# A two-block transformer kernel: opening, attention order and the place of half units

## The reference

```
x = x + 0.5 * swiglu(rmsnorm(x), wg, wu, wd)        # 1024 -> 2816 -> 1024
h = rmsnorm(x) @ w_in
o = concat(mla_mixer(h_a), nsa_mixer(h_b), diff_mixer(h_c))
x = x + o @ w_out
x = x + 0.5 * swiglu(rmsnorm(x), wg2, wu2, wd2)
```

## Time and profile before

| | |
|---|---|
| Median of 3 runs | 1830.25 us (1827.8 to 1834.87) |
| The profiled execution | 1835.67 us |
| Its span, first to last instruction | 1833.9 us |
| Busy in the span | PE 1711.5, DVE 1158.1, ACT 867.2, POOL 112.8 us |
| PE's mean granted clock | 0.953 of full speed |

### The profile page before, as it was taken

One profiled execution on the slowest core, in us unless ns is written; L12 is line 12 of the kernel. 1 busy time (PEld: TensorE's weight loads), 2 busy tenths in 40 slices (PEclk: granted clock), 3 DMA queues, 4 the chain that ended last, 5 costly groups with the idle time before them and its releaser, 6 DMA issues.

```text
span 1833.9 us, 30713 instructions
## 1 busy us (share of the span) xinstructions
PE 1711.5 (93%) x12072; PEld 1567.2 (85%) x12072; DVE 1158.1 (63%) x1286; ACT 867.2 (47%) x1035; POOL 112.8 (6%) x89
## 2 busy tenths in 40 slices
PE   3999999999999799999999999979998979999997
PEld 3999978778999799997877899968997967787785
DVE  6655566446555465557544655557755758888887
ACT  3433443345343443443434544346643537666675
POOL 0000031001000100003100100001201000000000
PEclk9999999799999899999968999989988989999999
DMA  7655731024555655564102455635532368998993
GB/s 214 197 189 178 188 116 47 24 70 143 189 195 183 161 184 190 193 165 138 36 12 82 148 185 181 194 109 159 163 115 69 113 232 293 319 346 306 345 330 121
DMA packets 237690, 312.96 MB, mean 171 GB/s; under 512 B 50900, under 2 KB 176148, under 8 KB 237604
## 3 DMA queue, kind: packets, MB, share of 16 engines
q1 hardware_dynamic: 237604, 311.82, 52.5%
HBM read 310.75 MB, written 1.05 MB: 170 GB/s over the span
## 4 chain that ended last, share of the span: by engine, by line
issue 51%; PE 37%; DVE 5%; POOLq 2%; POOL 2%; ACT 1%; DVEq 1%; DMA 0%; SPq 0%; ACTq 0%
PE psum L406 6%; PE psum L408 6%; PE psum L407 6%; PE psum L2520 3%; PE psum L2519 3%; PE psum L2521 3%; PE psum L2542 2%; PE psum L2543 2%; PE psum L2544 2%; PE psum L2478 1%; POOLq L1383 1%; POOL TMP L416 1%; DVE unit_low L398 1%; POOLq L422 1%; POOL QCOS L1396 1%
## 5 line engine op out<-in xcount | busy, mean ns | idle before, releaser
L406 PE MATMUL psum<-UH,unit_high 128*128 128x256 f32 x1888 | 546.0, 289 | 37.4 <-DVE UL L452 34.7
L398 DVE TENSOR_TENSOR unit_low<-unit_raw,unit_high 128x2048 fp32r<-128x2048 f32 (+1 forms) x186 | 427.3, 2298 | 226.4 <-ACT unit_high L392 223.8
L407 PE MATMUL psum<-UL,unit_high 128*128 128x256 f32 x1888 | 538.5, 285 | 0.0
L408 PE MATMUL psum<-UH,unit_low 128*128 128x256 f32 x1888 | 537.7, 285 | 0.0
L392 ACT ACTIVATE unit_high<-unit_raw 128x2048 fp32r<-128x2048 f32 (+1 forms) x186 | 347.7, 1870 | 151.0 <-PE psum L408 145.8
L406 PEld LDWEIGHTS psum<-UH,unit_high 128*128 128x128 f32 x1888 | 365.2, 193 | 44.5 <-DVE UL L452 37.9
L407 PEld LDWEIGHTS psum<-UL,unit_high 128*128 128x128 f32 x1888 | 363.9, 193 | 1.6 <-issue 1.4
L408 PEld LDWEIGHTS psum<-UH,unit_low 128*128 128x128 f32 x1888 | 365.1, 193 | 0.0
L2262 DVE TENSOR_TENSOR unit_low<-unit_raw,unit_high 128x2048 fp32r<-128x2048 f32 x99 | 222.4, 2287 | 29.3 <-ACT unit_high L2258 29.3
L406 PE MATMUL psum<-HH,unit_high 128*128 128x256 f32 x704 | 196.6, 279 | 5.8 <-DVE HL L584 5.8
L407 PE MATMUL psum<-HL,unit_high 128*128 128x256 f32 x704 | 197.0, 280 | 0.0
(11 more groups left out here) (481 smaller groups left out, 2562.3 us busy)
## 6 DMA issues: line engine op xcount, KB each, us to landing
unit_raw<-in_ffn_wg SPq DMA_DIRECT2D x44, 1024.0 KB
unit_raw<-in_ffn_wu SPq DMA_DIRECT2D x44, 1024.0 KB
unit_raw<-in_ffn_wd SPq DMA_DIRECT2D x44, 1024.0 KB
unit_raw<-in_w_in SPq DMA_DIRECT2D x36, 1024.0 KB
unit_raw<-in_expert_w_gate SPq DMA_DIRECT2D x34, 1024.0 KB, 7.0
unit_raw<-in_expert_w_up SPq DMA_DIRECT2D x33, 1024.0 KB, 7.6
unit_raw<-in_expert_w_down SPq DMA_DIRECT2D x32, 1024.0 KB, 6.7
unit_raw<-in_w_out SPq DMA_DIRECT2D x10, 1024.0 KB
```

What stands on the lines that cost most here:

```text
L398: dve.tensor_tensor(low[s][:, 0:w], raw[s][:, 0:w], high[s][:, 0:w].bitcast(F32), ALU.subtract).then_inc(unit_low, 1)
L406: pe.matmul(dst, wh, xh, start=start, stop=False, skip_group_check=True)
L407: pe.matmul(dst, wh, xl, start=False, stop=False, skip_group_check=True)
L408: return pe.matmul(dst, wl, xh, start=False, stop=stop, skip_group_check=True)
```

## The change

- **Opening.** SP issues only the frequencies, the positions, the identity and `x` ahead of unit 0; the vectors and the rest of the constants (13 DMAs) go to ACT's queue. PE transposes `x` first. DVE folds the angles once into a new tile `ARG`; the cosine becomes sin(quarter turn - |ARG|), made on ACT together with the sine inside the first dense layer (`trig`), in both layers. ACT copies half of `x`. The five casts and the gain products move into DVE's dense layer (`vectors`), in both layers.
- **Small loads.** They move from ahead of unit 2 to behind the third step of the dense layer's loads, in both layers.
- **Last step.** Each dense layer's last step has its own `HH_LAST` and `HL_LAST` (in `PROJ`'s tiles 8 to 11); ACT and DVE make them before they split the next unit, and ACT's wait on `unit_used` goes.
- **Seams.** At a layer's top, and between first dense layer and mixer, the splits of the next units come after `UH`, `UL` and the residual instead of ahead of them.
- **Mixer.** Rotation 1 moves up behind the uq matmuls; `h1` and the rest of the compression move ahead of head 0 and into the first heads, `s_cmp` ahead of head 4. Units 6, 7 and 8 are issued in two halves with two or three other pieces between them, output tiles 1 and 2 likewise. ACT's and DVE's orders and the marks follow.

New helpers: `first_half(j)` waits for unit j and for `p{j-2}` and issues 24 matmuls, `second_half(j)` the other 24. The core of the diff, cut:

```diff
+        ARG = own("one", "ARG", [P, 3, T])
         COS = own("one", "COS", [P, 3, T])
         SIN = own("one", "SIN", [P, 3, T])
+        PROJ_AT = parts["one"]
         PROJ = own("one", "PROJ", [P, 18, T])
+        HH_LAST = nc.alloc_sbuf_tensor_at("HH_LAST", [P, 2, T], F32R, offset=PROJ_AT + 8 * T * 4)
+        HL_LAST = nc.alloc_sbuf_tensor_at("HL_LAST", [P, 2, T], F32R, offset=PROJ_AT + 10 * T * 4)
...
-        def late_norm_act(act, i, gain, free=None):
+        def late_norm_act(act, i, gain, free=None, unit=None):
...
+            if unit is not None:
+                split_high(act, *unit)
...
+            def steps(a_, b_):
+                with sp.Fori(a_, b_) as it:
+                    up_units(wg, g + it, c0 - 1, it)
+                    up_units(wu, g + it, c0, it)
+                    down_unit(g + it, c0 + 1, it - 1)
+
             if small:
+                steps(1, 4)
                 small_loads(sp, l)
-            with sp.Fori(1, STEPS) as it:
-                up_units(wg, g + it, c0 - 1, it)
-                up_units(wu, g + it, c0, it)
-                down_unit(g + it, c0 + 1, it - 1)
+                steps(4, STEPS)
+            else:
+                steps(1, STEPS)
...
+                hh, hl = (HH_LAST, HL_LAST) if last else (HH, HL)
...
+            if trig:
+                act.wait_ge(start_dve, SM.at("angles"))
+                act.activation(COS[:, :, :], ARG[:, :, :], ACT.Abs)
+                act.activation(SIN[:, :, :], ARG[:, :, :], ACT.Sin)
+                act.drain()
+                act.activation(COS[:, :, :], COS[:, :, :], ACT.Sin, scale=-1.0, bias=quarter[:, :]).then_inc(tables, 1)
...
             split_high(act, g, c0 + MLP_UNITS - 1)
+            high_step(last, HH_LAST)
             split_high(act, g, c0 + MLP_UNITS)
-            act.wait_ge(unit_used, used(g, c0 + 3 * last + 1))
-            high_step(last)
...
+            if vectors:
+                dve.wait_ge(start_act, 1)
+                dve.tensor_tensor(GG[:, :], GC[:, 48:56], GC[:, 56:64], ALU.mult)
+                dve.tensor_tensor(GFE[:, :], GC[:, 48:56], GC[:, 48:56], ALU.mult)
+                dve.drain()
+                dve.tensor_scalar(GFE[:, :], GFE[:, :], EPS, None, ALU.add)
+                dve.wait_ge(consts_in, 32)
+                for dst, src in CASTS:
+                    dve.tensor_copy(dst[:, :], K[:, src])
...
             product(g, c0 + 3 * last, last)
+            low_step(last, HH_LAST, HL_LAST)
             split_low(dve, g, c0 + MLP_UNITS)
-            low_step(last)
...
-        ROT_BANK = (3, 2, 3, 2, 1)
+        ROT_BANK = (3, 7, 2, 2, 2)
...
+            pe.wait_ge(DM.sem, DM.at("p3", l))
+            rotation(1, K_RB).then_inc(PM.sem, PM.inc("rot1"))
...
-            rotation(1, K_RB).then_inc(PM.sem, PM.inc("rot1"))
             pe.wait_ge(LM.sem, LM.at("kpe", l))
             scores(0)
             scores(1)
             rotation(2, K_RC).then_inc(PM.sem, PM.inc("rot2"))
-            unit(6)
-            pe.wait_ge(AM.sem, AM.at("mla_v", l))
-            head(0)
-            head(1)
-            pe.wait_ge(DM.sem, DM.at("rot1", l))
-            rotation(3, K_RC).then_inc(PM.sem, PM.inc("rot3"))
-            unit(7)
-            head(2)
-            head(3)
...
+            first_half(6)
+            pe.wait_ge(AM.sem, AM.at("mla_v", l))
+            head(0)
+            head(1)
...
+            second_half(6)
+            head(2)
+            head(3)
...
+            first_half(7)
...
             mm.then_inc(PM.sem, PM.inc("s_cmp"))
-            pe.wait_ge(AM.sem, AM.at("vb_b", l))
-            rotation(4, K_RB).then_inc(PM.sem, PM.inc("rot4"))
-            head(8)
-            head(9)
+            head(4)
+            head(5)
+            second_half(7)
+            head(6)
+            head(7)
...
             mm.then_inc(PM.sem, PM.inc("t_cmp"))
-            head(10)
+            first_half(8)
+            head(8)
...
+            head(9)
+            second_half(8)
+            head(10)
+            pe.wait_ge(DM.sem, DM.at("p8", l))
...
+            rotation(4, K_RB).then_inc(PM.sem, PM.inc("rot4"))
             tokens_to_features((0, 1), 0)
             tokens_to_features((2,), 1).then_inc(PM.sem, PM.inc("ot012"))
+            head(11)
+            pe.wait_ge(AM.sem, AM.at("vb_b", l))
+            out_tile(0, "low2")
             head(12)
-            pe.wait_ge(DM.sem, DM.at("cmp_out", l))
-            out_tile(0, "low2")
             head(13)
+            out_tile(1, "low2", range(0, 4))
             head(14)
-            out_tile(1, "low2")
+            out_tile(1, "low2", range(4, KT))
             head(15)
+            out_tile(2, "low2", range(0, 4))
             head(16)
             pe.wait_ge(DM.sem, DM.at("o_diff", l))
             tokens_to_features((6, 7), T_BANK).then_inc(PM.sem, PM.inc("ot67"))
-            out_tile(2, "low2")
+            out_tile(2, "low2", range(4, KT))
             pe.wait_ge(DM.sem, DM.at("low67", l))
             head(17)
...
+            act.wait_ge(PM.sem, PM.at("h1", l))
+            act.activation(H1[:, :, :], psum[0:64, 3, 0:128].rearrange("p (n f) -> p n f", n=2)[:, :, 0:30], ACT.Exp, scale=-1.0)\
+               .then_inc(AM.sem, AM.inc("h1e"))
             high_of(8)
             head(0)
             head(1)
...
+            dve.wait_ge(tables, l + 1)
...
             rotated(0)
             low_of(6)
+            rotated(1)
             projected(4)
...
         def start_sp(sp):
-            sp.dma_start(K[:, :], a["constants"]).then_inc(consts_in, 16)
-            row = 0
-            for name, n in GAINS:
-                sp.dma_start(PROJ[row:row + n, 12, 0:P], a[name]).then_inc(vectors_in, 16)
-                row += n
-            row = 0
-            for name, n in TAPS:
-                sp.dma_start(PROJ[row:row + n, 13, 0:P], a[name]).then_inc(vectors_in, 16)
-                row += n
-            sp.dma_start(POS_I[:, :], a["positions"].to_broadcast([P, T])).then_inc(vectors_in, 16)
+            sp.dma_start(K[:, K_INV], a["constants"][:, K_INV]).then_inc(angles_in, 16)
+            sp.dma_start(POS_I[:, :], a["positions"].to_broadcast([P, T])).then_inc(angles_in, 16)
+            sp.dma_start(K[:, K_ID], a["constants"][:, K_ID]).then_inc(identity_in, 16)
             sp.dma_start(XIN, a["x"].rearrange("(t p) d -> p t d", p=P)).then_inc(inputs_in, 16)
...
         def start_pe_program(pe):
             pe.nop().then_inc(unit_used, 3)
-            pe.wait_ge(consts_in, 16)
-            pe.wait_ge(vectors_in, 16 * (len(GAINS) + len(TAPS) + 1))
-            pe.transpose(psum[:, 0, 0:88], PROJ[0:88, 12, 0:P], K[0:88, 0:88])
-            pe.transpose(psum[:, 0, P:P + 104], PROJ[0:104, 13, 0:P], K[0:104, 0:104]).then_inc(start_pe, 1)
+            pe.wait_ge(identity_in, 16)
             pe.wait_ge(inputs_in, 16)
             for k in range(KT):
                 for t in range(2):
                     mm = pe.transpose(psum[:, 1 + k // 2, (k % 2) * T + t * P:(k % 2) * T + t * P + P], XIN[:, t, k * P:k * P + P], K[:, K_ID])
-            mm.then_inc(start_pe, 1)
+                if k % 4 == 3:
+                    mm.then_inc(start_pe, 1)
+            pe.wait_ge(vectors_in, 16 * (len(GAINS) + len(TAPS)))
+            pe.transpose(psum[:, 0, 0:88], PROJ[0:88, 12, 0:P], K[0:88, 0:88])
+            pe.transpose(psum[:, 0, P:P + 104], PROJ[0:104, 13, 0:P], K[0:104, 0:104]).then_inc(start_pe, 1)
+            pe.wait_ge(consts_in, 32)
...
         def start_act_program(act):
-            act.wait_ge(start_dve, SM.at("angles"))
-            act.activation(SIN[:, :, :], SIN[:, :, :], ACT.Sin)
-            act.activation(COS[:, :, :], COS[:, :, :], ACT.Sin).then_inc(start_act, 1)
+            row = 0
+            for name, n in GAINS:
+                act.dma_start(PROJ[row:row + n, 12, 0:P], a[name]).then_inc(vectors_in, 16)
+                row += n
+            row = 0
+            for name, n in TAPS:
+                act.dma_start(PROJ[row:row + n, 13, 0:P], a[name]).then_inc(vectors_in, 16)
+                row += n
+            for part in (slice(K_ID.stop, K_INV.start), slice(K_INV.stop, K_COLS)):
+                act.dma_start(K[:, part], a["constants"][:, part]).then_inc(consts_in, 16)
+            act.wait_ge(start_pe, 1)
+            for j in range(2):
+                act.activation(X[:, 2 * j:2 * j + 2, SEQ], two(psum[:, 1 + j, :]), ACT.Copy).then_inc(x_ready, 1)
+            split_high(act, 0, 0)
+            act.wait_ge(start_pe, 3)
+            act.activation(GC[:, 0:88], psum[:, 0, 0:88], ACT.Copy)
+            act.activation(CW[:, :], psum[:, 0, P:P + 104], ACT.Copy).then_inc(start_act, 1)
+            act.drain()
...
             ang, turns = ROT[:, 0:3, :], ROT[:, 3:6, :]
-            for dst, quarter in ((SIN, 0.0), (COS, 0.25)):
-                dve.tensor_scalar(turns, ang, 1.0 / TWO_PI, quarter, ALU.mult, ALU.add)
+            dve.tensor_scalar(turns, ang, 1.0 / TWO_PI, None, ALU.mult)
+            dve.drain()
```

(53 more changed lines are left out.)

207 lines of the change are left out of this document (100 added, 107 removed).

## The result

The changed kernel takes 1781.95 us (median of 4 runs, 1780.72 to 1790.5) against 1831.72 for the kernel before, measured beside it (4 runs): a ratio of 0.974, with a 95% interval of 0.970 to 0.978. The forecast was 1778, the range 1762 to 1801. The profiled execution took 1780.79 us, its span is 1779.0, 54.9 us less than before.

A forecast was written before the change was run, and what follows sets the result against it. PE was taken to bound the kernel, through idle waits and stretches at low clock. The terms 15.5 + 5.8 + 2.8 + 4.5 + 24 + 1.5 - 2 = 52.1 us, from 1830.25, gave 1778 us, range 1762 to 1801.

The forecast's parts named there:

- Opening, 15.5: Start of the kernel: PE's first product at 18.3 us instead of 33.76, 15.5 us earlier; bounds 12 to 17.5.
- Last step, 5.8: Last step of each dense layer: PE's four waits for `HL` go, 5.8 us; bounds 4 and 5.8.
- Seam to the mixer, 2.8: First dense layer to mixer: PE's waits for `UL` go, 1.4 us per layer, 2.8 in all; bounds 0 and 4.6.
- Top of layer 2, 4.5: Start of layer 2: `UL` made ahead of unit 1's low part shortens PE's wait, 4.5 us; bounds 2.5 and 6.
- Mixer, 24 + 1.5: Both mixers: most falls of PE's clock go, 12 us per layer, 24; waits before head 16 go, 1.5.
- The fall left behind `s_cmp`: Mixer, behind the compressed scores: one clock fall of about 12 us stays, costing 5 us per layer.
- Small loads, -2: Dense layer's load queue: the moved block delays unit 11's load, PE waits 1 us per layer; bounds 0 and -6 per layer.
- Rival 3: Dense layer: small loads stall PE in full, 6 us per layer instead of 1, giving 1788 us; chance 0.12.
- a sign of being wrong: Dense layer: the prediction is wrong if PE waits for a load in the fourth or fifth step.
- its other signs: First product 18 to 19 us; `HL` waits within 0.3; layer 2's `UL` wait within 5; mixer clock 0.9, one fall.

The follow-up runs named there:

- experiment 3: Changed kernel with the last step's `HH` and `HL` made as before, without their own tiles: 1791.0 us, ratio 0.977 to the kernel before.
- Experiment 5: Changed kernel with the folds of the squares at the two seams made by DVE instead of POOL: 1779.3 us, ratio 0.973 to the kernel before.
- experiment 1: Changed kernel with the former mixer (order on PE, ACT, DVE and POOL, marks, rotation banks): 1810.5 us, ratio 0.987 to the kernel before.
- experiment 2: Two variants of the changed kernel: new mixer order with units and tiles whole, 1803.7 us; former mixer order with them in halves, 1808.4 us.

## Why the prediction was right, step by step

**Opening, 15.5.** 14.6 at the first product. `x` came 1.2 us sooner than I let it; the wait for unit 0 (2.23) and the table load (1.28) were not in the sum, though bounds of 12 to 17.5 held them. The table load stands in the trace of the kernel before as well and could have been read there. Tables and casts in the dense layer cost nothing: in layer 2, which makes them too, PE is 28.94 us ahead at unit 1 and 28.93 at unit 10.

**Last step, 5.8.** Some 6.5 by experiment 3. The restart behind each wait was left out.

**Seam to the mixer, 2.8.** This step failed. It gave -0.2 in each layer where 1.4 was forecast. The waits for `UL` did shrink (PE is 1.08 us further ahead behind unit 0), but the split moved behind `UL` runs beside POOL's fold, the norm comes late and PE waits 1.44 us for it. The step said "behind a split of 2.3 us" and asked what stood before `UL`, not what the split would stand beside at its new place. Experiment 5 shows it and gives back 1.6 to 1.8 us at each seam.

**Top of layer 2, 4.5.** The first product came 5.96 us sooner beyond the last step's share (with the `HL` wait just before it 7.2 by the table), and 3.07 were given back in unit 0, so 2.9 net, inside the bounds. `UL` stands beside the folds there. And of the 10.2 us at the low clock 5.6 lay in PE's idle time before and 0.7 now, so more of them falls on PE's work. Both are only read from the traces, not tried.

**Mixer, 24 + 1.5.** 13.4 and 18.8 by the table, 32.2. The mechanism was right: the clock, with some 1.5 us of waits (experiment 1), and long pieces bring the falls back (experiment 2), where the new order alone is worth 8 of the 26.5 us and the halves alone nothing. Why a stretch of small products brings a fall stays open: these runs change the order and the cuts, not the products. The fall left behind `s_cmp` was put at 12 us; in 14 mixers traced with this order and these halves it was 10.2 us nine times, 6.8 twice and 0 three times, 7.5 on average. The profiled execution had one of the three, which alone is worth 4.5 us. 0.42 per slow us fits: 10.2 us of them cost 4.5. So the size of this step is luck in part. The Trainium skill (TensorE: Matmul & The Clock Gate, HAM oscillation) puts falls down to idle gaps of PE; the trace does not agree, with 66.93 of 67.00 us busy around the one of layer 1.

**Small loads, -2.** Mis-sized: -5.76, within the bounds of 0 to -12. The stall was 2.73 and 1.24 us where 1 was said, and in layer 1 the clock fell at its end. Rival 3 in its size, though not in full. The prediction had named this as a sign of being wrong, a wait of PE for a load in the fourth step of the dense layer, and that sign came; it cost 3.8 us more than forecast. Of its other signs, the first product came at 19.16, just beyond 18 to 19, and layer 2 had no fall where one was expected; the rest came as said.

**What was in no step.** Some 4 us of the 54.9 lie in the second block, whose code is the same. It comes in two forms in the traces: granted clock 0.97 or 0.92 over the same work, here by windows of the kernel before and of the changed one:

```profile
1374.00:1499.00 125.00, 110.13 (x809) 102.56 (x808) 76.30 (x86) 48.98 (x84) 7.16 (x3) 0.92 0.41 141
```
```profile
1324.00:1445.00 121.00, 106.25 (x809) 98.83 (x808) 76.48 (x87) 49.03 (x84) 7.17 (x3) 0.97 0.42 149
```

Six of the 14 traces have the long form, with former and new mixers among them; what decides is open. The medians, 49.8 us apart, hold less of such luck than the two profiles.

Summed: 52.1 forecast, 49.8 by the medians, 54.9 by the profiles. In the profiles seam and loads were 7.0 us too high, last step and mixer 7.5 too low; part of why the sum fits is that they cancel.

## What to carry over

Where PE slows without waiting, look for long stretches of small products and put big ones between them. Here the new order alone gave little, the cut units alone nothing, and both together most of the gain; cutting finer gave no more, and new waits. When an instruction of DVE is moved, ask which POOL instruction it will run beside as well as who waits for it. A block of small DMAs in a queue of prefetched loads should be shorter than the lead; three groups of 6 cost nothing where one of 18, once in each layer, cost 5.8 us. Compare by landmarks in two traces before believing or dismissing a few us in a median.

## What had not been expected of the hardware

- A POOL `tensor_tensor` of 128x512 took 1.27 us alone and 3.35 beside DVE's splits; a `UL` of DVE took 1506 ns instead of 472 beside a fold.
- The same loop body, same order, gave a fall of 10.2 us in one layer and none in the next, with PE busy in 66.93 of 67.00 us in the layer that fell.
- The part of a fall that lies in PE's idle time costs PE nothing: before, of 10.2 us at the top of layer 2, 5.6 passed before the first product.
- PE's first products run at the low clock in all 14 traces. Before, 13 of them start 0.2 us apart until 36.7, and 0.12 from there on; in the changed kernel 18, until 23.2. The traces' clock record shows it only where it begins early enough; in the changed kernel it begins at 23.2, so the mean clock leaves these out. In six traces it lasts longer or the first product comes sooner, and unit 0 takes 0.5 to 0.9 us more than in the changed kernel. At unit 2 nothing of that is left: the norm's wait of 0.60 us is not there.
